# First modulation in four column steps, ten units computed chunk by chunk, in a one-core fp32 decoder layer

## The chip, the core and the metric

The kernel runs on one core of a Trainium2 chip. The metric is the device time of the whole program in microseconds (us). PE is TensorE, ACT ScalarE, DVE VectorE, POOL GpSimd, SP the engine whose queue issues most transfers. A number such as L1267 is a line of the kernel.

## What is computed

One decoder layer, 256 tokens (`S`) of 1024 features (`D`), all float32. A modulation vector of 6 x 1024 numbers comes from `c`; its first third (shift and scale) acts on the normalised input of the mixer. The mixer projects that input by `w_in` (6216 columns) into queries, keys and values of three attention branches, an indexer and gates.

```python
c_act = jax.nn.silu(c)
mod = c_act @ w_ada[l] + b_ada[l]
sh1, sc1, g1, sh2, sc2, g2 = [m[:, None, :] for m in jnp.split(mod, 6, axis=-1)]
h = rms_norm(x, g_pre_mix[l]) * (1.0 + sc1) + sh1
y = hybrid_mixer(h, w_in[l], b_gate[l], w_proj_sb[l], w_proj_moba[l], w_proj_dsa[l], w_o[l], slopes)
x = x + g1 * rms_norm(y, g_post_mix[l])
h = rms_norm(x, g_pre_ffn[l]) * (1.0 + sc2) + sh2
y = swiglu(h, w_up[l], w_down[l])
x = x + g2 * rms_norm(y, g_post_ffn[l])
```

In the mixer: 5 heads of plain causal attention (`mb`), 6 of stick-breaking attention (`sb`), 5 that see only the 64 keys with the highest index score (`ds`); the scores come from 8 small index heads ("logits").

## The kernel before

**Precision.** Every weight and activation is cut into a high part (an ACT copy to fp32r) and a low part (a DVE subtraction), and a product is three matmuls: high x high, high x low, low x high (`three`, L1265 to L1269). So each weight block that arrives costs ACT and DVE one pass each (`cut_hi` L635, `cut_lo` L931) before PE can use it.

**Mixer units.** `w_in` is loaded in 17 column blocks (all 1024 rows each) through two buffers `raw[0]` and `raw[1]`; block b may be loaded when block b-2 has been cut. The 51 units of `UNITS` are the output tiles: unit 0 (block 0, index keys and weights), 1 to 4 (block 1, index queries), 5 and 6 (block 2, queries of mb), 7 to 9 (block 3, keys of mb and a last head), 10 and 11 (block 4, values), and so on to the 24 gate units 27 to 50. A unit of features takes 24 matmuls: 8 chunks of 128 input features, three matmuls each. Each engine runs through the units in program order, and tables by unit number place everything else between them: `LOGIT_PAIR_AT` (index logits), `ROUND_AT` (eight top-k rounds on DVE), `SCORES_AT`, `EXP_AT`, `SECOND_AT`, `OUTPUT_AT` (attention of one head every two units), `ADA_UNIT` (the other two thirds of the modulation: 16 parts of 1 MB, loaded by POOL and accumulated on DVE at L1001 to L1007), `PIECES_AT` (the cuts of block b+1 during the units of block b).

**Start.** The first third of the modulation needs 8 MB of `w_ada`: a quarter of its rows at a time goes to `raw[0]`, `raw[1]` and two `ada_end` buffers, all issued by SP ahead of `w_in`. PE multiplies it (L1274), DVE copies the row (L1013), PE turns it (L1307), DVE makes scale and shift columns, ACT and DVE apply them to the turned x (L734, L1038) and cut the result (L738, L1046), and unit 0 starts. All 2048 sums end with the last rows.

**Tail of the mixer.** Blocks 17 to 20 are the projection weights; SP may issue block 19 (L461, L466) only after the last cut of block 17, which stands at unit 50. Then POOL merges the branches (L604, L607), `w_o`, and the feed-forward loop.

## Time and profile before

| | |
|---|---|
| median of 3 runs | 475.29 us (472.71 to 476.57) |
| the profiled execution: its own time | 475.56 us |
| its span in the trace | 473.4 us |
| mean granted TensorE clock | 0.983 of full |

The profile shows one execution. Its span is 2.2 us shorter than its own time, by what lies ahead of and behind the traced work. Rows of the trace are in a section below; a start time in them is counted from the beginning of the span.

### The profile page before, as it was taken

How to read it: one execution, taken by the hardware profiler on the slowest of the kernel's cores; microseconds unless marked ns; L12 is line 12 of the kernel's file. 1: busy time of each engine (PE TensorE's matmuls, PEld its weight loads, DVE VectorE, ACT ScalarE, POOL GpSimd, SP SyncE). 2: the span in 40 equal slices, each digit the busy share in tenths (PEclk: the TensorE clock that was granted, in tenths of full speed). 3: DMA queues.
4: the chain of work that ended last, by engine and by line, in shares of the span. 5: the costliest groups of instructions: out<-in, count | busy, mean ns of one | idle time of the engine just before them, and what ended most of it. 6: DMA issues, size and time to landing. Idle time of an engine off the chain costs nothing.

```text
span 473.4 us, 7656 instructions
## 1 busy us (share of the span) xinstructions
PE 442.6 (93%) x2927; PEld 390.4 (82%) x2927; DVE 315.3 (67%) x542; ACT 237.4 (50%) x417; POOL 55.0 (12%) x84
## 2 busy tenths in 40 slices
PE   0959999999999999999988999999999999999994
PEld 0629999999889999998886899888888888888883
DVE  3047579768399959673799447785855675585545
ACT  6046555546576655567465237554444253444232
POOL 2001001200023140000399100000000000000000
PEclk9969999999999999999999999999999999999998
DMA  8996898596856675752677900998475556620002
GB/s 296 426 367 212 271 312 298 180 316 226 325 182 206 238 267 206 251 162 76 198 267 280 369 17 2 329 362 271 133 237 177 190 164 200 237 94 1 1 0 89
DMA packets 56817, 99.85 MB, mean 211 GB/s; under 512 B 5212, under 2 KB 41684, under 8 KB 53716
## 3 DMA queue, kind: packets, MB, share of 16 engines
q1 hardware_dynamic: 54132, 81.62, 50.3%
q0 software_dynamic: 2656, 17.84, 10.7%
q8 instruction: 19, 0.31, 0.3%
q14 instruction: 10, 0.08, 0.0%
HBM read 98.39 MB, written 1.06 MB: 210 GB/s over the span
## 4 chain that ended last, share of the span: by engine, by line
PE 81%; DMA 5%; POOL 4%; DVE 3%; ACT 2%; SPq 2%; issue 1%; DVEq 0%; POOLq 0%; PEldq 0%; ACTq 0%
PE psum L1267 16%; PE psum L1567 16%; PE psum L1268 15%; PE psum L1269 15%; PE psum L1568 8%; DMA ada_end<-in_w_ada_dram 4%; PE psum L1531 3%; DVE wlo L931 1%; POOL xn L607 1%; POOL bufp L604 1%; PE psum L1418 1%; POOL hcut L598 1%; PE psum L1357 1%; PE psum L1355 1%; PE psum L1389 1%
## 5 line engine op out<-in xcount | busy, mean ns | idle before, releaser
L1567 PE MATMUL psum<-hcut,whi 128*128 128x512 f32 x320 | 111.9, 395 | 0.0
L1267 PE MATMUL psum<-hcut,whi 128*128 128x256 f32 (+1 forms) x360 | 106.0, 294 | 3.5 <-DVE hcut L1046 2.7
L1268 PE MATMUL psum<-hcut,whi 128*128 128x256 f32 (+1 forms) x360 | 102.4, 284 | 0.0
L1269 PE MATMUL psum<-hcut,wlo 128*128 128x256 f32 (+1 forms) x360 | 102.3, 284 | 0.0
L931 DVE TENSOR_TENSOR wlo<-raw,whi 128x1024 fp32r<-128x1024 f32 (+4 forms) x84 | 78.0, 957 | 24.6 <-ACT whi L635 24.3
L1568 PE MATMUL psum<-hcut,wlo 128*128 128x256 f32 x320 | 88.9, 278 | 0.0
L635 ACT ACTIVATE whi<-raw 128x1024 fp32r<-128x1024 f32 (+4 forms) x84 | 66.3, 821 | 22.7 <-DMA raw<-in_w_in_dram 16.5
L1267 PEld LDWEIGHTS psum<-hcut,whi 128*128 128x128 f32 (+1 forms) x360 | 68.9, 191 | 8.6 <-issue 3.2
L1567 PEld LDWEIGHTS psum<-hcut,whi 128*128 128x128 f32 x320 | 60.0, 188 | 14.1
L1268 PEld LDWEIGHTS psum<-hcut,whi 128*128 128x128 f32 (+1 forms) x360 | 69.0, 192 | 0.0
L1269 PEld LDWEIGHTS psum<-hcut,wlo 128*128 128x128 f32 (+1 forms) x360 | 68.9, 191 | 0.0
L1568 PEld LDWEIGHTS psum<-hcut,wlo 128*128 128x128 f32 x320 | 60.1, 188 | 0.4
L1196 DVE TENSOR_TENSOR dlo<-draw,dhi 128x2048 fp32r<-128x2048 f32 x11 | 25.1, 2291 | 44.0 <-ACT dhi L840 44.0
L1191 DVE TENSOR_TENSOR wlo<-raw,whi 128x1024 fp32r<-128x1024 f32 x40 | 47.1, 1220 | 4.5 <-ACT whi L833 4.5
L833 ACT ACTIVATE whi<-raw 128x1024 fp32r<-128x1024 f32 x40 | 39.8, 1046 | 3.1 <-DMA raw<-in_w_up_dram 3.1
L1007 DVE SCALAR_TENSOR_TENSOR acc<-xn,csil,acc 128x2048 f32<-128x2048 f32 x14 | 32.9, 2350 | 7.0 <-DMA xn<-in_w_ada_dram 6.9
L840 ACT ACTIVATE dhi<-draw 128x2048 fp32r<-128x2048 f32 x11 | 20.9, 1912 | 31.1 <-PE psum L1269 31.1
L878 ACT ACTIVATE fsil<-fsil 128x256 f32<-128x256 f32 x20 | 8.4, 418 | 52.8 <-DVE fsil L1208 52.8
L1268 PE MATMUL psum<-dlo,fhi 128*128 128x512 f32 x88 | 34.3, 390 | 0.0
L1267 PE MATMUL psum<-dhi,fhi 128*128 128x512 f32 x88 | 34.3, 390 | 0.0
L1269 PE MATMUL psum<-dhi,flo 128*128 128x512 f32 x88 | 34.3, 390 | 0.0
L1268 PE MATMUL psum<-wlo,hcut 128*128 128x320 f32 (+2 forms) x80 | 28.2, 353 | 0.0
(180 smaller groups left out, 697.8 us busy)
## 6 DMA issues: line engine op xcount, KB each, us to landing
raw<-in_w_up_dram SPq DMA_DIRECT2D x22, 1024.0 KB, 7.5
xn<-in_w_ada_dram POOLq DMA_DIRECT2D x16, 1024.0 KB, 5.2
raw<-in_w_in_dram SPq DMA_DIRECT2D x7, 2048.0 KB, 9.1
draw<-in_w_down_dram SPq DMA_DIRECT2D x11, 1024.0 KB, 5.1
raw<-in_w_in_dram SPq DMA_DIRECT2D x4, 1280.0 KB, 7.1
raw<-in_w_in_dram SPq DMA_DIRECT2D x3, 1536.0 KB, 7.0
raw<-in_w_ada_dram SPq DMA_DIRECT2D x2, 2048.0 KB, 9.8
ada_end<-in_w_ada_dram SPq DMA_DIRECT2D x4, 1024.0 KB, 17.0
```

Source lines behind the costliest of these rows:

```text
L635: act.activation(block_view(whi[b % 2], b)[0:p, chunks, cols], block_view(raw[r % 2], b)[0:p, chunks, cols], ACT.Copy).then_inc(w_hi, 1)
L833: act.activation(block_view(whi[slot], B_FFN)[:, 2 * q:2 * q + 2, :], block_view(raw[slot], B_FFN)[:, 2 * q:2 * q + 2, :], ACT.Copy).then_ ...
L840: act.activation(dhi[slot][:, :, :], draw[slot][:, :, :], ACT.Copy).then_inc(d_hi, 1)
L931: dve.tensor_tensor(block_view(wlo[b % 2], b)[0:p, chunks, cols], block_view(raw[r % 2], b)[0:p, chunks, cols], block_view(whi[b % 2], b)[ ...
L1007: ins = dve.scalar_tensor_tensor(acc[:, :], ada_part, csil[:, k:k + 1], acc[:, :], ALU.mult, ALU.add)
L1191: dve.tensor_tensor(block_view(wlo[slot], B_FFN)[:, 2 * q:2 * q + 2, :], block_view(raw[slot], B_FFN)[:, 2 * q:2 * q + 2, :], block_view(w ...
L1196: dve.tensor_tensor(dlo[slot][:, :, :], draw[slot][:, :, :], dhi[slot][:, :, :].bitcast(F32), ALU.subtract).then_inc(d_lo, 1)
L1267: pe.matmul(dst, a[0], b[0], start=first, stop=False)
L1268: pe.matmul(dst, a[0], b[1], start=False, stop=False)
L1269: return pe.matmul(dst, a[1], b[0], start=False, stop=last)
L1567: pe.matmul(dst[:, :], wh, hcut[:, k, :, :].rearrange("p a s -> p (a s)"), start=k == 0, stop=False)
L1568: mm = pe.matmul(dst[:, S:2 * S], wl, hhi[:, k, :], start=False, stop=k == KC - 1)
```

## The change

The first third of the modulation is now made in four steps p of 256 features. The sum of a feature runs over all rows of `w_ada`, so a step loads all 1024 rows of 2 x 256 columns (`load_ada`, 2 MB in pieces of 1 KB). Between the steps SP loads, for each chunk k of 128 input features, the rows of blocks 0 to 3 that belong to it (`load_chunk`: 1224 columns, 627 KB in rows of 2336, 1024 and 256 bytes). PE computes units 0 to 9 side by side: for each chunk three matmuls for each of ten units, in halves of banks 0 to 4. x is now turned without its norm; 1/rms is applied as a row (`rootrow`) together with the scale. Small vectors are loaded from ACT's queue instead of SP's. The copies of units 0 to 9 out of the banks, and the four logit pairs, come after the last chunk; heads start one unit later, and the tables of sums and top-k rounds are new. A helper `warm_up` (transposes of a constant) is defined and not called.

```diff
+FIRST_BLOCK, FIRST_UNIT = 4, 10
+Q_COLS, CHUNK_COLS = W_IX + HD + H_IX, W_IX + HD + H_IX + 2 * W_MB
+CHUNK_BASE = [W_IX, 0, Q_COLS, Q_COLS + W_MB - HD]
...
-HEAD_START = 13
+HEAD_START = 14
...
-LOGITS_AT = {5 + h: h for h in range(H_IX)}
-LOGIT_PAIR_AT = {5 + 2 * j: j for j in range(H_IX // 2)}
+LOGIT_PAIR_AT = {FIRST_UNIT + j: j for j in range(H_IX // 2)}
 TOPK_ROUNDS = TOPK // 8
-ROUND_AT = {25 + r: r for r in range(TOPK_ROUNDS)}
+ROUND_AT = {u: r for r, u in enumerate([18, 19, 24, 28, 29, 30, 32, 34])}
...
-    for b in range(N_MIX):
+    for b in range(FIRST_BLOCK, N_MIX):
...
-ADA_UNIT = [2, 4, 6, 9, 12, 15, 18, 22, 25, 28, 31, 34, 37, 40, 43, 46]
+ADA_UNIT = [12, 14, 16, 19, 21, 23, 25, 27, 29, 31, 33, 35, 37, 41, 43, 45]
...
+        def first_place(u):
+
+            return bank[u // 2][:, S * (u % 2):S * (u % 2 + 1)]
+
+        def mod_columns(p):
+
+            return bank[6 + p % 2][:, 0:4]
...
+            def load_ada(p):
+
+                if p >= 2:
+                    sp.wait_ge(gemv, p - 1)
+                for a in range(2):
+                    sp.dma_start(ada[p % 2][:, :, a, :], ada_dram[:, :, D * a + 2 * P * p:D * a + 2 * P * (p + 1)]).then_inc(ada_in[p], 16)
+
+            def load_chunk(k):
+
+                if k >= 6:
+                    sp.wait_ge(w_hi, 2 * (k - 2))
+                    sp.wait_ge(w_lo, 2 * (k - 2))
+                view = chunk_view(raw, None, k)
+                sp.dma_start(view[:, 0:Q_COLS], in_dram[:, k, O_QIX:O_QIX + Q_COLS]).then_inc(chunk_in[k], 16)
+                heads = in_dram[:, k, O_QMB:O_QMB + 2 * W_MB].rearrange("p (a n) -> p a n", a=2)
+                pairs, last = view[:, Q_COLS:CHUNK_COLS - P], view[:, CHUNK_COLS - P:CHUNK_COLS]
+                sp.dma_start(pairs.rearrange("p (a n) -> p a n", a=2), heads[:, :, 0:W_MB - HD]).then_inc(chunk_in[k], 16)
+                sp.dma_start(last.rearrange("p (a n) -> p a n", a=2), heads[:, :, W_MB - HD:W_MB]).then_inc(chunk_in[k], 16)
+
...
+                if b < FIRST_BLOCK + 2:
+
+                    sp.wait_ge(w_hi, (6, 2 * KC)[b - FIRST_BLOCK])
+                    sp.wait_ge(w_lo, (6, 2 * KC)[b - FIRST_BLOCK])
+                else:
+                    sp.wait_ge(w_hi, 4 * (b - 1))
+                    sp.wait_ge(w_lo, 4 * (b - 1))
...
+            for k in range(KC):
+                if k % 2 == 0:
+                    load_ada(k // 2)
+                load_chunk(k)
+            for b in range(FIRST_BLOCK, B_FFN):
+                load(b)
...
-                    pool.wait_ge(h_lo, 4)
+                    pool.wait_ge(tmp_ready, KC)
...
+                    if b < FIRST_BLOCK + 2:
+                        act.wait_ge(chunk_done, 3 * (b - FIRST_BLOCK + 1))
...
+            for w, k0 in ((b_ada, VEC_ADA), (g_pre_mix, VEC_PRE_MIX), (b_gate, VEC_GATE),
+                          (g_post_mix, VEC_POST_MIX), (g_pre_ffn, VEC_PRE_FFN), (g_post_ffn, VEC_POST_FFN)):
+                n = w.shape[0] * w.shape[1] // P
+                act.dma_start(vec_rows[k0:k0 + n, :], w.rearrange("l (k p) -> (l k) p", p=P)).then_inc(vec_in, 16)
...
+            act.wait_ge(x_in[0], 16)
+            act.activation(squares0[0], xt[:, 0, :], ACT.Square, accum_out=ssq[:, 0, 0:1]).then_inc(ss_ready, 2)
+            for i in (0, 2):
+                act.wait_ge(x_raw_turned, i + 1)
+                act.activation(h32[:, 2 * i:2 * i + 2, :], turned_two(i), ACT.Copy).then_inc(x_kept_act, 1)
+            act.wait_ge(var_ready, 2)
+            act.activation(root_[:, 0:TT], var[:, 0:TT], ACT.Sqrt).then_inc(sqrt_ready, 2)
+            for k in range(KC):
+                act.wait_ge(chunk_in[k], 48)
+                act.activation(chunk_view(whi, end_hi, k), chunk_view(raw, None, k), ACT.Copy).then_inc(w_hi, 2)
+                if k % 2 == 0:
+                    act.wait_ge(gemv, k // 2 + 1)
+                    if k:
+                        act.wait_ge(mod_turned, k // 2)
+                    act.activation(mrow[:, :], bank[5][:, :], ACT.Copy).then_inc(row_kept, 1)
+                act.wait_ge(tmp_ready, k + 1)
+                act.activation(hhi[:, k, :], htmp[k % 2], ACT.Identity, bias=col[0][:, k:k + 1]).then_inc(chunk_hi, 1)
+                if k == 1:
+                    act.preload_act_table_set("natural_log_exp_and_others")
+                cut_hi(FIRST_BLOCK, q)
+            for u in range(FIRST_UNIT):
+                take_unit(u)
+            for u in range(FIRST_UNIT, N_UNITS):
...
+            def chunk_cut_lo(k):
+                dve.wait_ge(w_hi, 2 * (k + 1))
+                dve.tensor_tensor(chunk_view(wlo, end_lo, k), chunk_view(raw, None, k),
+                                  chunk_view(whi, end_hi, k).bitcast(F32), ALU.subtract).then_inc(w_lo, 2)
+            def pair_columns(p):
+                dve.wait_ge(mod_turned, p + 1)
+                cols = slice(2 * p, 2 * p + 2)
+                scale, base = col[0][:, KC:2 * KC][:, cols], VEC_ADA + KC + 2 * p
+                then(dve.tensor_tensor(scale, mod_columns(p)[:, 2:4], vecs[:, base:base + 2], ALU.add))
+                then(dve.tensor_tensor(scale, scale, vecs[:, VEC_PRE_MIX + 2 * p:VEC_PRE_MIX + 2 * p + 2], ALU.mult))
+                then(dve.tensor_tensor(col[0][:, cols], mod_columns(p)[:, 0:2], vecs[:, VEC_ADA + 2 * p:VEC_ADA + 2 * p + 2], ALU.add))
+                dve.sem_inc(mod_ready, 1)
+            def chunk_scaled(k):
...
+                if k >= 2:
+                    dve.wait_ge(chunk_hi, k - 1)
+                dve.scalar_tensor_tensor(htmp[k % 2], h32[:, k, :], col[0][:, KC + k:KC + k + 1], rootrow,
+                                         ALU.mult, ALU.mult).then_inc(tmp_ready, 1)
+            def chunk_rest(k):
+                dve.wait_ge(chunk_hi, k + 1)
+                dve.scalar_tensor_tensor(hlo[:, k, :], htmp[k % 2], col[0][:, k:k + 1], hhi[:, k, :].bitcast(F32),
+                                         ALU.add, ALU.subtract).then_inc(chunk_lo, 1)
+            for k in range(KC):
+                chunk_cut_lo(k)
+                if k % 2 == 0:
+                    pair_columns(k // 2)
+                chunk_scaled(k)
+                chunk_rest(k)
+            dve.sem_inc(col_ready, 1)
+                cut_lo(FIRST_BLOCK, q)
...
-            def first_products():
-                for k in range(KC):
...
-                    mm = product(k, buf[:, ADA_COLS * (k % 2):ADA_COLS * (k % 2 + 1)])
...
+            def row_products(p):
+                pe.wait_ge(ada_in[p], 32)
+                if p == 0:
+                    pe.wait_ge(c_ready, 2)
+                else:
+                    pe.wait_ge(row_kept, p)
+                w = ada[p % 2]
+                for half in range(2):
+                    for j in range(4):
+                        mm = pe.matmul(bank[5][32 * j:32 * j + 32, :], crep[:, 4 * half + j, :],
+                                       w[:, 4 * half + j, :, :].rearrange("p a n -> p (a n)"),
+                                       start=half == 0, stop=half == 1, tile_position=(0, 32 * j))
+                mm.then_inc(gemv, 1)
+            def turn_row(p):
+                pe.wait_ge(row_kept, p + 1)
+                if p == 0:
+                    pe.wait_ge(pick_ready, 1)
+                    pe.wait_ge(x_kept_act, 1)
+                if p < 2:
+                    pe.wait_ge(x_kept_dve, 1)
+                else:
+                    pe.wait_ge(mod_ready, p - 1)
+                for n in range(4):
+                    mm = pe.matmul(mod_columns(p)[:, n:n + 1], mrow[:, P * n:P * (n + 1)], pick[:, :], start=True, stop=True)
+                mm.then_inc(mod_turned, 1)
...
+            def first_unit(u, k):
+                b, what, c0, n, dest = UNITS[u]
+                base = CHUNK_COLS - P if what == "last head" else CHUNK_BASE[b] + c0
+                wh, wl = [chunk_view(x, ends, k)[:, base:base + n] for x, ends in ((whi, end_hi), (wlo, end_lo))]
+                dst = first_place(u)[0:n, :]
+                pe.matmul(dst, wh, hhi[:, k, :], start=k == 0 and u in (1, 2, 4, 6, 8), stop=False, skip_group_check=True)
+                pe.matmul(dst, wh, hlo[:, k, :], start=False, stop=False, skip_group_check=True)
+                return pe.matmul(dst, wl, hhi[:, k, :], start=False, stop=k == KC - 1, skip_group_check=True)
...
+                if u < FIRST_UNIT + 2:
+                    pe.wait_ge(unit_read, 2 * (u - FIRST_UNIT + 1))
...
+            for i in range(4):
+                turn_raw_x(i)
+            pe.transpose(bank[4][:, 0:VEC_END], vec_rows[:, :], ident[0:VEC_END, 0:VEC_END]).then_inc(vec_turned, 1)
+            row_products(0)
+            pe.wait_ge(root_ready, 1)
+                mm = pe.transpose(bank[3][:, S + P * t:S + P * (t + 1)], rinv[:, t:t + 1].to_broadcast([P, P]), ident[:, :])
+            mm.then_inc(root_turned, 1)
+            turn_row(0)
+            for k in range(KC):
+                pe.wait_ge(w_hi, 2 * (k + 1))
+                pe.wait_ge(w_lo, 2 * (k + 1))
+                pe.wait_ge(chunk_hi, k + 1)
+                pe.wait_ge(chunk_lo, k + 1)
+                for n in range(FIRST_UNIT):
+                    u = n ^ 1 if k == 0 and n < 2 else n
...
+                    mm = first_unit(u, k)
+                    if k == KC - 1:
+                        mm.then_inc(units, 1)
+                    elif n == FIRST_UNIT - 1:
+                        mm.then_inc(chunk_done, 1)
+                    if n == 1 and k % 2 and k < KC - 1:
+                        turn_row(k // 2 + 1)
+                if k % 2 == 0 and k < KC - 2:
+                    row_products(k // 2 + 1)
...
+                        pe.wait_ge(unit_read, 8)
+                    if j == 1:
+                        pe.wait_ge(unit_read, 10)
```

What the order of instructions shows. On PE, from the last turned tile to the first unit, before (xn and ident hold the diagonal and identity, raw and ada_end the modulation weights, crep silu(c), mrow the summed row, hcut the cut input, whi and wlo the weight parts):

```order
L1324 MATMUL psum<-xn,xt 128x128 x16
L1274 MATMUL psum<-raw,crep 32x512 x16
L1274 MATMUL psum<-ada_end,crep 32x512 x16
L1307 MATMUL psum<-ident,mrow 128x128 x4
L1267 MATMUL psum<-hcut,whi 72x256
L1268 MATMUL psum<-hcut,whi 72x256
L1269 MATMUL psum<-hcut,wlo 72x256
```

And in the changed kernel on PE, from the last unit of chunk 0 to the third unit of chunk 1:

```order
L1401 MATMUL psum<-hcut,whi 128x256
L1402 MATMUL psum<-hcut,whi 128x256
L1403 MATMUL psum<-hcut,wlo 128x256
L1362 MATMUL psum<-ada,crep 32x512 x8
L1401 MATMUL psum<-hcut,whi 72x256
L1402 MATMUL psum<-hcut,whi 72x256
L1403 MATMUL psum<-hcut,wlo 72x256
L1401 MATMUL psum<-hcut,whi 128x256
L1402 MATMUL psum<-hcut,whi 128x256
L1403 MATMUL psum<-hcut,wlo 128x256
L1378 MATMUL psum<-pick,mrow 128x1 x4
```

The 32 products that stood in one piece ahead of all units are four groups of 8; the next step's group follows an even chunk, and its turn (L1378) stands behind two units of the odd chunk, so that eight units remain behind it.

On ACT, chunks 1 and 2 of the changed kernel (before, the ten copies of units stood among the cuts and no unit waited for them in one piece):

```order
L768 ACTIVATE whi<-raw 128x1224
L775 ACTIVATE hcut<-bufp,col 128x256
L777 ACT_TABLE_LOAD
L768 ACTIVATE whi<-raw 128x1224
L773 ACTIVATE mrow<-psum 128x512
L775 ACTIVATE hcut<-bufp,col 128x256
```

The copy of the row (L773) stands behind the cut of the chunk (L768), which waits for that chunk's arrival.

On SP, the first step and its two chunks in the changed kernel, up to the next step:

```order
L467 DMA ada<-in_w_ada_dram 128x8x256 x2
L475 DMA raw<-in_w_in_dram 128x584
L478 DMA raw<-in_w_in_dram 128x2x256
L479 DMA raw<-in_w_in_dram 128x2x64
L475 DMA raw<-in_w_in_dram 128x584
L478 DMA raw<-in_w_in_dram 128x2x256
L479 DMA raw<-in_w_in_dram 128x2x64
L467 DMA ada<-in_w_ada_dram 128x8x256 x2
```

Before, six whole transfers of `w_ada` stood here, and `w_in` behind all of them.

## Rows read from the trace of the kernel before

**Rows 1.** The page: busy time, slices of PE, chain by engine.

```profile
PE 442.6 (93%) x2927; PEld 390.4 (82%) x2927; DVE 315.3 (67%) x542; ACT 237.4 (50%) x417; POOL 55.0 (12%) x84
...
PE   0959999999999999999988999999999999999994
...
PE 81%; DMA 5%; POOL 4%; DVE 3%; ACT 2%; SPq 2%; issue 1%; DVEq 0%; POOLq 0%; PEldq 0%; ACTq 0%
```

**Rows 2.** Timeline of PE, 0 to 75 us: start, time, engine, line, tiles.

```profile
11.66 6.16 PE L1324 MATMUL psum<-xn,xt 128*128 128x128 f32 x32 [4.09 <-DVE xn L957]
17.75 3.64 PE L1274 MATMUL psum<-raw,crep 128*32 128x512 f32 x32
...
27.01 1.93 PE L1274 MATMUL psum<-ada_end,crep 128*32 128x512 f32 x8 [1.52 <-DMA ada_end<-in_w_ada_dram]
29.85 1.11 PE L1307 MATMUL psum<-ident,mrow 128*128 128x128 f32 x4 [0.91 <-DVE mrow L1013]
33.66 0.46 PE L1267 MATMUL psum<-hcut,whi 128*72 128x256 f32 x1 [2.70 <-DVE hcut L1046]
...
68.08 0.41 PE L1267 MATMUL psum<-whi,hcut 128*128 128x320 f32 x1
```

**Rows 3.** The chain that ended last, pieces of 0 to 54 and 214 to 262 us.

```profile
1.27 0.42 SPq L432
...
6.94 20.03 DMA ada_end<-in_w_ada_dram
...
53.52 0.42 PE psum L1355 x4
53.94 0.43 PE psum L1357 x4
...
220.01 1.59 ACT qk L803
221.59 0.53 ACT whi L635
...
223.53 0.37 SPq L461
```

**Rows 4.** Stretches: start:end, length, busy (x instructions) by engine, PEclk, DMA share, GB/s.

```profile
8.00:26.00 18.00, 12.52 (x88) 7.58 (x88) 2.58 (x13) 2.26 (x6) 0.00 (x0) 1.00 1.01 423
26.80:33.60 6.80, 3.05 (x12) 0.91 (x12) 3.67 (x11) 2.93 (x8) 0.00 (x0) 0.50 1.07 368
33.66:37.05 3.39, 3.38 (x16) 3.39 (x17) 2.79 (x5) 3.33 (x7) 0.00 (x0) 0.50 0.64 206
34.00:35.00 1.00, 1.00 (x7) 1.00 (x6) 1.00 (x2) 0.97 (x3) 0.00 (x0) 0.50 1.10 353
37.05:68.08 31.03, 30.73 (x253) 28.85 (x251) 22.15 (x28) 17.27 (x33) 2.28 (x4) 1.00 0.83 276
46.00:48.00 2.00, 2.00 (x19) 2.00 (x18) 0.23 (x2) 0.20 (x1) 0.00 (x0) 1.00 1.24 343
60.00:80.00 20.00, 20.00 (x157) 18.54 (x156) 16.30 (x23) 10.96 (x22) 1.05 (x2) 1.00 0.86 287
140.00:160.00 20.00, 20.00 (x159) 18.44 (x158) 19.65 (x44) 12.28 (x22) 5.32 (x15) 1.00 0.73 252
```

**Rows 5.** Who waited for whom, PE alone, 68 to 220 us.

```profile
PE psum L1267 <- DVE wlo L931: 0.5, 1, 0.5
```

**Rows 6.** Timeline of ACT, 0 to 75 us.

```profile
32.70 0.55 ACT L734 ACTIVATE xn<-psum,col 128x256 f32<-128x256 f32 x1
...
36.05 3.89 ACT L635 ACTIVATE whi<-raw 128x1024 fp32r<-128x1024 f32 x4
```

**Rows 7.** Timeline of DVE, 0 to 75 us.

```profile
29.10 0.69 DVE L1013 COPY mrow<-psum 128x512 f32<-128x512 f32 x1 [17.12 <-PEq L1290]
...
31.21 0.17 DVE L987 SCALAR_TENSOR_TENSOR col<-col,vecs 128x8 f32<-128x8 f32 x1
...
37.12 5.23 DVE L931 TENSOR_TENSOR wlo<-raw,whi 128x1024 fp32r<-128x1024 f32 x5 [0.26 <-ACT whi L635]
...
53.11 2.35 DVE L1007 SCALAR_TENSOR_TENSOR acc<-xn,csil,acc 128x2048 f32<-128x2048 f32 x1 [3.69 <-DMA xn<-in_w_ada_dram]
```

More of the change, by code:

```diff
@@ L1032, in _ @@
[L1032 to L1047 removed]
+            dve.wait_ge(ident_ready, 1)
```

327 lines of the change are left out of this document (143 added, 184 removed).

## The prediction, made before the changed kernel ran

> **What bounds the kernel now.** I read the page first. PE is busy for 442.6 of 473.4 us, its slices show 9 everywhere but at the start, around 220 to 260 us and at the end, and 81% of the chain that ended last is PE [rows 1]. So time can only be won where PE waits. I then read PE's timeline of the start, to see what stands ahead of the first unit: PE turns x, multiplies the first modulation as its parts arrive, and begins unit 0 at 33.66; the first block that the change leaves alone (unit 10) begins at 68.08 [rows 2]. The chain says why: a transfer of `w_ada` issued at 6.94 lands 20.03 later, at 26.97 [rows 3], and behind it come the last products, the copy of the row, its turn and the columns, 6.7 us to the first unit [rows 2]. The stretches show the queue full meanwhile (8 to 26 us: DMA share 1.01, 423 GB/s) and TensorE's granted clock: 0.50, its 1.2 GHz level, from 26.8 until 37.05, after thin work on PE (3.05 us busy of 6.8) and until unit 0 had kept it busy for 3.39 us; from then on 1.00, 2.4 GHz [rows 4]. Last I asked who PE waits for from 68 to 220 us: 0.5 us in all [rows 5]. What reaches unit 10 earlier therefore arrives earlier at 220 us too, unless something else becomes late.
>
> **What the change does to the start: transfers.** The same 8.39 MB of `w_ada` and 5.01 MB of `w_in` must arrive before unit 9 can end, but products and units now run beside the transfers. The price of the pieces changes. `w_ada` came in rows of 8 KB at 423 GB/s; pieces of 1 KB moved at 353 (34 to 35 us, block 2), and a mixture with pieces of 256 bytes at 343 (46 to 48 us) [rows 4]. I take 353 for the steps and 343 for the chunks: 2.10 MB / 353 = 5.9 us a step, 0.627 MB / 343 = 1.8 us a chunk, 4 x 5.9 + 8 x 1.8 = 38.4 us. SP issues x at 1.27 [rows 3]; x (1.05 MB) is through at about 5, and I add 1 us from last byte to landing. Arrivals: step 0 at 11.9, chunks 0 and 1 at 13.8 and 15.6, step 1 at 21.5, chunk 2 at 23.4, step 2 at 31.1, chunk 4 at 33.0, step 3 at 40.8, chunk 6 at 42.6, chunk 7 at 44.4. The waits of SP (`gemv`, cuts of chunks 3 and 4) are met before the queue runs dry, and the small vectors are on ACT's queue. The slow bound is 287 GB/s, the mean of 60 to 80 us with DMA share 0.86 [rows 4]: 46.7 us instead of 38.4.
>
> **The first chunk.** Behind chunk 0 at 13.8 stand the cut of 1224 columns (ACT, 4 cuts of 1024 took 3.89: 1.2 us [rows 6]), the copy of the row (DVE took 0.69 [rows 7]; ACT the same, I take 0.7), four turns of one column (no such row; four transposes at the low clock took 1.11 [rows 2]; bounds 0.4 and 1.1, I take 0.8), three small columns on DVE (0.17 and a semaphore each [rows 7]: 0.7), then scaled, high, low part (three of about 0.5, as L734's 0.55 [rows 6]) and handovers of 0.2: PE starts chunk 0 at about 19.
>
> **PE from there.** 240 matmuls. At the low clock 16 took 3.39 us, 0.21 each, at the high one about 0.12 (1.00 shows 253 records in 31.03 us, which hold three logit pairs too) [rows 4]: 28.8 us, and 1.5 more for a first 3.4 us at 1.2 GHz, since PE has idled before chunk 0. Three of the four product groups now stand in this stretch: 32 records took 3.64 [rows 2], so 16 take 1.8, together 5.5. Three turns at 0.7: 2.1. Sum 37.9: PE ends unit 9 at 19 + 37.9 = 56.9. Whether PE waits in between: the turn of step 1 needs chunk 2 (23.4), its cut, the products (26.1) and the copy (26.8), and PE reaches it at 26.8; the 24 matmuls behind it (2.9 us) cover columns, scale, cut and rest (2.3). For step 2 the same reckoning gives row and PE both at 36.6, for step 3 46.3 and 46.3. Transfers and PE are in balance, so each microsecond by which transfers are later costs most of a microsecond. In one chunk ACT works 1.2 + 0.5 + 0.35 = 2.1 us and DVE 1.4 (five cuts took 5.23 [rows 7]) + 1.0 + 0.35 = 2.8, against PE's 4.7: hidden; if the low parts of a chunk were late, PE would stand for the difference.
>
> **Behind the last chunk.** Block 4 comes after chunk 7 (1.31 MB, 3.8 us: 48.2) and is cut by 56; unit 10 waits for two copies only, the others (about 5 us of ACT) are done at 60.5, before the second logit pair asks for all ten at 65. Block 5 is issued when chunk 7 is cut (51.5), shares the queue with the first 1 MB part and is there by 60; its last low cut ends near 66.7, unit 12 asks for it about then. Unit 10 starts at 57.0. But three logit pairs, 0.42 + 0.43 each [rows 3], that stood ahead of 68.08, and the turn of the index weights (0.25), now stand behind: 2.8 us. Compared like with like the start wins 68.1 - 57.0 - 2.8 = 8.3 us.
>
> **What moves into the middle.** Four parts of the modulation (2.35 each on DVE [rows 7], the first less) and five logit sums leave the first ten units and are added to units 10 to 45: some 12 us of DVE work. Before, DVE had 16.3 of 20 us in 60 to 80 and 19.65 of 20 in 140 to 160, and there too PE did not idle [rows 4]. Over 36 units of some 3.7 us (133 us) that is 9 points more of DVE's time in the mean, and more ahead of unit 28, where three of the eight top-k rounds now stand as well; in return 140 to 160 us gets lighter. A part of 1 MB has 7.4 us for its load now. I charge 0.5 us; the bound above is the work that finds no room, 5 us.
>
> **The tail.** Heads are a unit later, so the last output stands at unit 49. On ACT its copy (0.4 and a wait of 0.8) comes between unit 49's copy and the sigmoid batch (1.59), and behind that is the cut (0.53) that lets SP issue block 19 at 223.53 [rows 3]. That is 1.2 later after unit 49, but PE comes to unit 49 0.8 earlier: +0.4.
>
> **Sum.** 473.4 - 8.3 + 0.5 + 0.4 = 466.0 of span, plus the 2.2 around it 468.2; the profiled execution is 0.3 above the median of the runs shown, so I say **468.0**, 1.5% less.
>
> **A rule against it.** The trace shows the low clock after thin work on PE [rows 4]. The Trainium skill, page "TensorE: Matmul & The Clock Gate", section "HAM oscillation — how this bites in real kernels", says that a matmul kernel which waits for a transfer behind each group of matmuls starts every group at the low clock again. By the row, the clock is low once, for 3.4 us; by the rule, each chunk pays, which is the first rival's result.
>
> **Rivals.** (1) *The clock stays low, slower.* Nothing keeps PE busy before chunk 0 and while rows are awaited. If all 240 matmuls and the groups ran at 1.2 GHz: 240 x 0.09 = 21.6 less the 1.5 counted, and 3 x 2 us of products (8 records took 1.93 at the low clock [rows 2]), +26: 494. It decides from three chunks at the low clock on (2.7 each: 476). For it: low clock after 3.05 of 6.8 us busy. Against: at 1.2 GHz a chunk takes 6.4 us, longer than its share of transfers (4.8), so PE would be busy all the time, and the row shows the rise after 3.4 such us. 0.10, with all other ways to be slower 0.12. (2) *Transfers bind.* At 287 GB/s everything is 8.3 us later and the start wins about 1: 475; at 320 GB/s 4 us are lost: 471.5. For it: many pieces of 1 KB and 256 bytes with the short rows of `w_in`; against: 353 and 343 were measured with such pieces. 0.15. (3) *Given back.* DVE finds no room in units 16 to 34, or the tail eats more: 470.5 to 474. For it: 19.65 of 20; against: 0.5 us of waits. 0.13. (4) The forecast and what lies near or below it (clock high at once, turns for 0.4: 464): 0.60.
>
> **How the numbers follow.** The forecast's own range is 464 to 471. Up to 475.5 come the transfers' and the middle's cases; below 463.5 I leave 0.06, above 475.5 0.13. About 1% (4.8 us) is what a measurement of this kernel can tell. Faster than 470.5: most of the forecast's cases, some of (3) and (2): 0.68. Slower than 480: 0.10. The rest, 0.22, within.
>
> **What would show it.** Right: the first L1401 near 19 us, unit 10 near 57, GB/s of 340 to 360 from 5 to 44, PEclk 0.5 for one stretch of some 3.4 us at chunk 0, block 19 issued near 216, the low cut with waits under 1 us on PE. Wrong: the first chunk behind 21; landings of steps more than 7 us apart beyond their two chunks; PEclk 0.5 in several chunks; PE waiting for `wlo` between 90 and 150 us, or the gap from unit 50 to the projections grown by more than 1 us.

## The result, and the profile after

The changed kernel takes 486.14 us (median of four runs, 483.34 to 488.63) against 475.93 us for the kernel before on the same chip: the ratio is 1.021, with a 95% interval of 1.012 to 1.031. It is slower by about 10 us where I had forecast 468.0. A second set of four runs of it gave 484.38 us and 1.021 (1.015 to 1.026). The profiled execution is the slowest of the first four (488.63 us), so the stretches below add up to somewhat more than the medians differ by.

The page of the changed kernel answers to [rows 1]: busy time, the slices of TensorE and of its granted clock, then the chain that ended last by engine.

```profile
PE 452.0 (93%) x2941; PEld 395.8 (81%) x2941; DVE 321.5 (66%) x550; ACT 237.8 (49%) x408; POOL 56.2 (12%) x84
...
PE   3699999999799997999979899989999999999994
...
PEclk9689999999979999999979999999999999999998
...
PE 58%; DMA 18%; DVE 13%; issue 4%; POOL 3%; ACT 3%; SPq 2%; DVEq 0%; ACTq 0%; POOLq 0%
```

The start fills its slices sooner (3, 6, 9 where there was 0, 9, 5), but the chain has changed character. 81% of it was PE; now it is 58% PE, 18% transfers and 13% DVE. There are also new 7s, where PE stands, in slices that were all 8s and 9s.

To see where the 13.5 us of span (486.9 against 473.4) arise, take three milestones: ACT's copies of units 14 and 50, and PE's first matmul by `w_up`, the up matrix of the feed-forward loop. Each fence holds rows of the timelines of ACT and PE, the first for the kernel before.

```profile
86.12 0.38 ACT L698 ACTIVATE qk<-psum 128x256 f32<-128x256 f32 x1 [2.81 <-PE psum L1269]
...
222.84 0.47 ACT L707 ACTIVATE qk<-psum,vecs 128x256 f32<-128x256 f32 x1 [0.73 <-PE psum L1269]
...
278.40 1.83 PE L1531 MATMUL psum<-xn,raw 128*128 128x128 f32 x15
```

The same three in the changed kernel:

```profile
81.48 0.39 ACT L734 ACTIVATE qk<-psum 128x256 f32<-128x256 f32 x1 [1.47 <-PE psum L1350]
...
229.35 0.47 ACT L744 ACTIVATE qk<-psum,vecs 128x256 f32<-128x256 f32 x1 [0.57 <-PE psum L1350]
...
288.05 2.17 PE L1664 MATMUL psum<-xn,raw 128*128 128x128 f32 x18
```

At unit 14 the changed kernel is 4.6 us ahead, at unit 50 it is 6.5 us behind, at the next milestone 9.7 behind and at the end 13.5. So the start did win; the units between lost 11.1 us; 3.1 us went between unit 50 and the up matrix, and 3.8 behind it.

One of these microseconds is no gain. Heads start one unit later now, so the scores of the first head stand ahead of unit 14 in the kernel before and behind it in the changed one. At unit 15 both have done them, and the lead is 3.6 us. These are the two copies of unit 15, first before, then changed.

```profile
89.00 0.38 ACT L698 ACTIVATE qk<-psum 128x256 f32<-128x256 f32 x1 [0.16 <-PE psum L1269]
```

```profile
85.41 0.38 ACT L734 ACTIVATE qk<-psum 128x256 f32<-128x256 f32 x1 [2.07 <-PE psum L1350]
```

Like with like, then, the start won 3.6 us, less than half of the forecast 8.3, and the units up to 50 lost 10.1. In the second profile of the changed kernel (span 481.9) the same two numbers are 3.8 and 9.2.

Next, who waited. The rows are: engine, tile and line that waited, for whom, us in all, times, the longest. First PE from 68 to 220 us, which was 0.5 us in all before [rows 5]; then DVE from 60 to 262 us (before: 3.3 us in all, the longest 1.1).

```profile
PE psum L1348 <- DVE wlo L973: 5.9, 4, 3.0
PE psum L1506 <- DVE smax L1199: 0.8, 1, 0.8
```

```profile
DVE acc L1046 <- DMA xn<-in_w_ada_dram: 15.1, 8, 4.5
```

DVE stands 15.1 us in `accumulate`, waiting for parts of the modulation; PE stands for the low cuts (`wlo`) that DVE makes in the same order of instructions. How one leads to the other is shown by the chain from 57 to 150 us: start, duration, what.

```profile
110.41 2.31 DVE acc L1046
112.71 0.28 issue
113.00 7.76 DMA xn<-in_w_ada_dram
120.78 2.36 DVE acc L1046
123.14 0.28 issue
123.43 6.29 DMA xn<-in_w_ada_dram
129.75 2.35 DVE acc L1046
132.10 1.15 DVE wlo L973
133.38 0.55 PE psum L1348
```

This is a closed loop. The parts have one buffer, so the next part is issued only when the last is accumulated: 2.35 us of DVE, 0.28 us to issue, and a load of 5.1 us at best, 6.29 and 7.76 here, where a weight block is on the queue too. One turn takes 7.75 us or more. The new table asks for a part every two units, mostly, and two units take 7.6 us in the mean of units 14 to 50 of the kernel before (7.1 to 7.8 for most gate units). At 133.38 PE has waited 2.96 us for the low cut behind the accumulation.

Stretches of the changed kernel follow (start:end, length, busy time and instructions of PE, PEld, DVE, ACT, POOL, then PEclk, DMA share, GB/s). They answer to [rows 4].

```profile
4.00:48.00 44.00, 35.42 (x245) 28.05 (x249) 20.20 (x43) 19.06 (x26) 0.00 (x0) 0.88 1.07 347
...
21.50:26.76 5.26, 5.26 (x24) 5.26 (x25) 2.31 (x3) 3.27 (x4) 0.00 (x0) 0.50 1.10 345
26.85:61.20 34.35, 34.35 (x289) 29.46 (x289) 18.63 (x31) 14.84 (x26) 0.69 (x1) 1.00 0.80 259
...
132.66:139.50 6.84, 6.12 (x21) 4.61 (x22) 4.21 (x6) 3.14 (x6) 0.28 (x1) 0.51 0.92 293
245.30:252.10 6.80, 6.06 (x28) 6.09 (x29) 3.45 (x8) 2.01 (x5) 4.97 (x5) 0.50 0.75 266
```

Two waits of PE, 2.96 us before 133.38 and 2.99 before 246.04, each go with 6.8 us at 1.2 GHz. The clock falls some 0.8 us before the wait ends, and for the 6.0 us of work behind it a matmul of 256 columns starts every 0.21 us instead of every 0.12.

Last, PE's timeline of the start, beside [rows 2].

```profile
13.37 3.48 PE L1362 MATMUL psum<-ada,crep 128*32 128x512 f32 x16 [3.46 <-DMA ada<-in_w_ada_dram]
...
17.57 1.05 PE L1378 MATMUL psum<-pick,mrow 128*128 128x1 f32 x8 [0.36 <-ACT mrow L773]
21.50 0.55 PE L1401 MATMUL psum<-hcut,whi 128*128 128x256 f32 x1 [2.88 <-DVE hcut L1117]
...
27.58 1.93 PE L1362 MATMUL psum<-ada,crep 128*32 128x512 f32 x16
...
61.22 0.31 PE L1348 MATMUL psum<-whi,hcut 128*128 128x320 f32 x1
```

Chunk 0 starts at 21.50 and unit 10 at 61.22; I had said 19 and 57. A first chunk behind 21, and PE waiting for `wlo` between 90 and 150 us, are two of the signs of being wrong that the prediction names.

### The profile page after: what moved, and what is told of

It is laid out like the page before. It is cut to its first block, busy times and chain, and to the rows that moved or that the text cites. A ratio compares the mean times of both kernels' runs of the same rounds, so it can differ in the third digit from the quotient of the medians.

```text
span 486.9 us, 7727 instructions
## 1 busy us (share of the span) xinstructions
PE 452.0 (93%) x2941; PEld 395.8 (81%) x2941; DVE 321.5 (66%) x550; ACT 237.8 (49%) x408; POOL 56.2 (12%) x84
## 4 chain that ended last, share of the span: by engine, by line
PE 58%; DMA 18%; DVE 13%; issue 4%; POOL 3%; ACT 3%; SPq 2%; DVEq 0%; ACTq 0%; POOLq 0%
PE psum L1700 14%; DMA xn<-in_w_ada_dram 9%; PE psum L1348 8%; PE psum L1350 8%; PE psum L1349 8%; PE psum L1701 7%; DMA raw<-in_w_in_dram 4%; DVE acc L1046 3%; PE psum L1664 3%; DVE wlo L973 3%; DMA ada<-in_w_ada_dram 2%; DMA raw<-in_w_up_dram 2%; PE psum L1362 2%; PE psum L1401 2%; PE psum L1402 1%
## 5 line engine op out<-in xcount | busy, mean ns | idle before, releaser
L1700 PE MATMUL psum<-hcut,whi 128*128 128x512 f32 x320 | 113.6, 399 | 1.7 <-DVE wlo L1272 1.7
L1701 PE MATMUL psum<-hcut,wlo 128*128 128x256 f32 x320 | 89.9, 281 | 0.0
L1348 PE MATMUL psum<-hcut,whi 128*128 128x256 f32 x280 | 82.9, 296 | 4.9 <-DVE wlo L973 4.9
L973 DVE TENSOR_TENSOR wlo<-raw,whi 128x768 fp32r<-128x768 f32 (+3 forms) x68 | 66.2, 1000 | 22.8 <-ACT whi L672 22.2
L1349 PE MATMUL psum<-hcut,whi 128*128 128x256 f32 x280 | 79.6, 284 | 0.0
L1350 PE MATMUL psum<-hcut,wlo 128*128 128x256 f32 x280 | 79.6, 284 | 0.0
L1700 PEld LDWEIGHTS psum<-hcut,whi 128*128 128x128 f32 x320 | 60.1, 188 | 17.0 <-issue 2.1
L672 ACT ACTIVATE whi<-raw 128x768 fp32r<-128x768 f32 (+3 forms) x68 | 55.7, 851 | 16.9 <-DMA raw<-in_w_in_dram 9.7
L1348 PEld LDWEIGHTS psum<-hcut,whi 128*128 128x128 f32 x280 | 54.0, 193 | 9.3 <-issue 5.9
L1701 PEld LDWEIGHTS psum<-hcut,wlo 128*128 128x128 f32 x320 | 60.4, 189 | 0.3
L1349 PEld LDWEIGHTS psum<-hcut,whi 128*128 128x128 f32 x280 | 54.1, 193 | 0.0
L1350 PEld LDWEIGHTS psum<-hcut,wlo 128*128 128x128 f32 x280 | 54.0, 193 | 0.0
L1046 DVE SCALAR_TENSOR_TENSOR acc<-xn,csil,acc 128x2048 f32<-128x2048 f32 x14 | 32.9, 2350 | 15.1 <-DMA xn<-in_w_ada_dram 15.1
## 6 DMA issues: line engine op xcount, KB each, us to landing
raw<-in_w_in_dram SPq DMA_DIRECT2D x6, 2048.0 KB, 10.1
```

The lines of the kernel that those rows point to most:

```text
L672: act.activation(block_view(whi[b % 2], b)[0:p, chunks, cols], block_view(raw[b % 2], b)[0:p, chunks, cols], ACT.Copy).then_inc(w_hi, 1)
L973: dve.tensor_tensor(block_view(wlo[b % 2], b)[0:p, chunks, cols], block_view(raw[b % 2], b)[0:p, chunks, cols], block_view(whi[b % 2], b)[ ...
L1046: ins = dve.scalar_tensor_tensor(acc[:, :], ada_part, csil[:, k:k + 1], acc[:, :], ALU.mult, ALU.add)
L1348: pe.matmul(dst, a[0], b[0], start=first, stop=False)
L1349: pe.matmul(dst, a[0], b[1], start=False, stop=False)
L1350: return pe.matmul(dst, a[1], b[0], start=False, stop=last)
```

## The experiments

All times are medians, ratios are to the kernel before on the same chip in the same sitting, with their 95% intervals. Four sittings: the first four kernels, the next four, the next four, the last three. The first kernel, the four combined ones, the shifted one and the last have ten executions each, the others four. Where two intervals overlap, a difference between these two kernels is suggested and not shown.

| kernel | us | ratio | interval |
|---|---|---|---|
| accumulations that do not wait | 478.25 | 1.009 | 1.006 to 1.011 |
| before, with the new table | 485.23 | 1.022 | 1.019 to 1.025 |
| wide table | 481.11 | 1.015 | 1.010 to 1.021 |
| parts in halves | 482.59 | 1.017 | 1.013 to 1.022 |
| old addresses | 483.95 | 1.022 | 1.017 to 1.027 |
| first part later | 483.79 | 1.021 | 1.018 to 1.024 |
| no wait, no accumulation | 475.59 | 1.004 | 0.999 to 1.009 |
| warm-up | 482.77 | 1.017 | 1.014 to 1.021 |
| combined | 474.55 | 1.001 | 0.999 to 1.004 |
| combined, parts whole | 476.43 | 1.004 | 1.001 to 1.006 |
| the changed kernel again | 484.38 | 1.021 | 1.015 to 1.026 |
| before, addresses shifted | 476.68 | 1.004 | 1.002 to 1.006 |
| combined, no accumulation | 471.73 | 0.995 | 0.992 to 0.997 |
| combined, old top-k table | 477.19 | 1.004 | 1.001 to 1.008 |
| before, halves and warm-up | 473.78 | 1.000 | 0.997 to 1.003 |

**Is it the wait for parts?** The first kernel takes the wait away and leaves every load where it is.

```diff
-                dve.wait_ge(part_in, 16 * (n + 1))
+                if n == 2 * KC - 1:
+                    dve.wait_ge(part_in, 16 * 2 * KC)
-                    ... acc[:, :], ada_part, ...
+                    ... acc[:, :], stale, ...        (stale is xt; in load_part POOL waits for the part before)
```

> The changed kernel, but the sixteen accumulations read another buffer and do not wait for their part; every part is still loaded, at the same point and into the same buffer (the sums of the second and third modulation are left out of the result). Theory 'part loop': the wait of VectorE for parts (15.1 us) and TensorE's waits behind it (8.9 us on the low cuts, two spells of 6.8 us at the low clock) go; the span falls by 8 to 12 us, to 475 to 478 us, and the milestones of units 23 to 50 return to those of before or earlier. Rival 'clock and start': the loss has other causes and this kernel stays within 3 us of the changed one (484 to 487).

It took 478.25 us: the wait costs 1.2% or some 6 us, and what was left of PE's waits from 60 to 262 us in it is this.

```profile
PE psum L1351 <- DVE wlo L975: 3.5, 3, 2.2
PE psum L1351 <- POOL hcut L637: 2.4, 3, 1.0
```

The time fell as the theory of the loop says, but by less than the 8 to 12 us expected, and to just above the expected range: the kernel without any wait for parts is still slower than before. (Its own POOL waits of 17.3 us for parts, which the edit added, may cost it a little.)

**Does the table alone do it?** The second kernel is the kernel before with the new table, and with the one line that must follow it, the unit after which POOL stores a gain (both as in the changed kernel).

```diff
-ADA_UNIT = [2, 4, 6, 9, 12, 15, 18, 22, 25, 28, 31, 34, 37, 40, 43, 46]
+ADA_UNIT = [12, 14, 16, 19, 21, 23, 25, 27, 29, 31, 33, 35, 37, 41, 43, 45]
...
-                if u == ADA_UNIT[KC] + 3:
+                if u == max(GAIN_AT) + 1:
                     store_gain(1)
```

> The kernel before with one edit: the units after which parts are accumulated are those of the changed kernel (12, 14, 16, 19, ... 45 in place of 2, 4, 6, 9, ... 46). Theory 'part loop': two units (7.1 to 7.5 us) are less than accumulate, issue and load (2.35 + 0.28 + 5.1 us or more), so this table alone slows the kernel before by 5 to 12 us. Rival 'the table is harmless, the loss comes of the start as a whole': within 2 us of before.

It is 2.2% slower than before, as much as the whole change. In it PE waits 6.5 us for low cuts between 60 and 262 us, and DVE 13.4 us for parts. The new start is not needed for the loss; the table is enough. Its 2.2% hold the wait and the crowding of DVE's work together, since it moves four accumulations from the first ten units to later ones; later kernels without the wait, or without the accumulations, ask for each alone.

**Can the loop be given room?** Two ways: more units between parts, or a shorter loop.

```diff
-ADA_UNIT = [12, 14, 16, 19, 21, 23, 25, 27, 29, 31, 33, 35, 37, 41, 43, 45]
+ADA_UNIT = [10, 12, 15, 17, 20, 22, 25, 27, 29, 32, 34, 37, 39, 42, 44, 46]
```

> The changed kernel with the sixteen accumulations spread over units 10 to 46, two or three units apart in turn (8.9 us on average in place of 7.4). Theory 'part loop': most of the 15.1 us of VectorE's waits and of TensorE's 8.9 us go; 474 to 478 us. If a two-unit distance now and then is already too much, 479 to 482. Rival: no change (485 to 487).

```diff
+                for i in range(2):
+                    if n and i:
+                        pool.wait_ge(acc_done, 2 * n)
+                    c0 = ADA_COLS * (1 + n // KC) + HALF * i
+                    pool.dma_start(ada_part[:, HALF * i:HALF * (i + 1)], ada_dram[:, n % KC, c0:c0 + HALF]).then_inc(part_in[i], 16)
...
+                    dve.wait_ge(part_in[i], 16 * (n + 1))
+                    ... accumulates columns HALF * i to HALF * (i + 1)
```

> The changed kernel with every part loaded and accumulated in two halves of 4 KB a partition: the first half is loaded again while the second is accumulated, so that the loop accumulate, issue, load is shorter (an estimate of 1.2 + 0.3 + 3.5 to 4.5 us for each half, in place of 7.75) at the same table of units. Theory 'part loop': 475 to 480 us. Rival 'the load is late because of the queue's and the memory's traffic, not because of its one buffer': 484 to 487.

Each gained less than I expected, some 2 to 3 us by the ratios, with intervals that overlap that of the changed kernel: 481.11, in the upper of the two ranges I had given, and 482.59, above its range of 475 to 480. In the wide table every second distance is still two units, and DVE waits 11.3 us for parts; with halves it waits 6.0 us, but the low cuts still come late (PE 4.4 us). Both point the same way as the first two runs, though neither gain is clear of noise by itself, and neither is the whole cure.

**Where is the rest?** Four single suspicions. The addresses first: the one new small buffer, `pick`, moves all later buffers by 32 bytes a partition.

```diff
-        pick = sb("pick", [P, 1])
         ...
         ssum = sb("ssum", [P, 2, TT], scope=mix)
+        pick = sb("pick", [P, 1], scope=mix)
```

> The changed kernel with the one new small buffer (pick, 32 bytes a partition) moved behind the others, so that the later buffers lie at the addresses they had before; no instruction changes otherwise. In the changed kernel each of the eight middle steps of the up and down matrices takes 16.79 us against 16.57 before, with the same instructions, and with the old program text and the new table it takes 16.57. Theory 'addresses': the steps return to 16.57 and the kernel gains 1.8 to 2.3 us, to 483 to 485. Rival 'place of the instructions in the program, or something else': the steps stay at 16.79, time 485 to 487.

```diff
                     pool.wait_ge(tmp_ready, KC)
+                    pool.wait_ge(raw_in[(FIRST_BLOCK + 1) % 2], RAW_ARRIVED[FIRST_BLOCK + 1])
```

> The changed kernel with the first part's load held back until the second weight block (block 5) has landed, so that the two do not share the queues. The block then lands 3 to 4 us earlier than at 66.35 and VectorE's idle 6.75 us before its cuts shrink. Theory 'part loop is what binds from unit 12 on': VectorE is free again before unit 12 either way, and the time stays within 1.5 us of the changed kernel. Rival 'the late block starts the delay': 3 to 4 us faster.

The third is the kernel without wait, with `accumulate` reduced to its semaphore for all parts but the first.

> As the kernel that accumulates from another buffer without waiting (478.25), but with fifteen of the sixteen accumulations left out (15 times 2.35 us = 35 us of VectorE; all parts are still loaded; the sums of the second and third modulation are wrong by that). It asks where the rest of the start's gain goes: that kernel was 5.8 us ahead of before at unit 12 and 2.0 behind it at the end. Theory 'VectorE's work itself is crowded, since three accumulations and three logit pairs moved from before unit 10 to behind it': TensorE's waits for low cuts (3.5 us) go too, and the time is 472 to 475. Rival: these waits come of the block loads or of the top-k steps, and it stays at 477 to 479.

```diff
             turn_row(0)
+            warm_up(12)
             for k in range(KC):
```

> The changed kernel with twelve transposes of the identity on TensorE in its idle stretch before chunk 0 (18.6 to 21.5 us), into a bank that chunk 0 starts afresh. The granted clock is at its lower level (1.2 GHz) from 13.2 to 16.6 and from 20.0 to 26.85 us. Theory 'clock': the low stretch behind 21.5 shortens or goes; chunk 0's 30 matmuls run at the upper level, unit 10 starts 2 to 3 us earlier than at 61.3; but since the later part loop binds, the end gains 1 us or less (484.5 to 486.5). Rival: the low stretch stays as long and nothing moves.

Addresses: the steps of the feed-forward loop did return to 16.57 us each. The median, 483.95, lies in the expected range, but so does that of the kernel beside it with the new addresses (483.79), and the ratio did not fall (1.022). An interval of 1.017 to 1.027 cannot show 0.4%, so the price was open until a later run. First part later: block 5 is cut from 64.3 instead of 66.35 us and DVE's idle stretch shrinks from 6.75 to 3.82 us, but the time stays (ratio 1.021); the delay does not start there. No accumulation: 475.59, just above the expected 472 to 475 and a further 0.4% below the first kernel, with intervals that overlap; suggestive, and taken up again below. Warm-up: PE's timeline shows what it does.

```profile
19.07 1.51 PE L1384 MATMUL psum<-ident 128*128 128x128 f32 x12
22.16 0.36 PE L1401 MATMUL psum<-hcut,whi 128*128 128x256 f32 x1 [1.59 <-DVE hcut L1117]
22.36 0.28 PE L1402 MATMUL psum<-hcut,whi 128*128 128x256 f32 x1
```

Chunk 0's matmuls take 0.28 us from the first, 0.12 apart, where they took 0.41, 0.21 apart. Chunk 0 started 0.7 us later in that execution and its product group still came at 25.89 instead of 27.58. The time is 482.77, 0.4% less than the changed kernel and more than I expected. But the intervals overlap, so it is not shown that the gain reached the end.

**Together, and the other way round.** The combined kernel has the wide table, the halves, the warm-up and the old addresses. Beside it ran the same with whole parts, the changed kernel again, and the kernel before with 32 bytes put in.

> The changed kernel with four edits together: parts in two halves, accumulations spread over units 10 to 46, the small new buffer behind the others (buffers at their old addresses), and twelve transposes of the identity before chunk 0. Measured one by one against before, in ratio: the changed kernel 1.021, wide table 1.015, halves 1.017, warm 1.017, and the address edit restores 16.57 us per middle step (about 2 us). If the effects add up as far as the waits allow: part waits gone (6 us), warm 1.7 us, addresses 2 us, so 474 to 476, ratio 0.999 to 1.004. Theory 'the crowded VectorE is what is left': not clearly faster than before, since about 3 us of accumulation work moved behind unit 10 remain. Rival: once nothing waits for parts the start's 6 us show and it is 470 or less.

> As the previous kernel but each part loaded whole, as in the changed kernel. Theory 'part loop': one part still needs 7.75 us or more, so with a distance of 7.4 us at every second part it waits some 10 us on VectorE in all and is 1.5 to 3 us slower than with halves. Rival 'the waits fall into VectorE's slack once the table is wide': within 1 us of it.

> The changed kernel once more (one comment differs), on the same chip as the kernels beside it, as their yardstick: 484 to 487, ratio 1.019 to 1.026.

```diff
+        spare = sb("spare", [P, 1])
         crep = sb("crep", [P, KC, 32])
```

> The kernel before with one unused small buffer (32 bytes a partition) in the place where the changed kernel has its new one, and nothing else. Theory 'addresses': the middle steps of the up and down matrices take 16.79 in place of 16.57 us and the time rises by 1.8 to 2.3 us (ratio 1.004 to 1.005). Rival 'the addresses matter only together with the changed program': no difference (within 0.5 us).

The combined kernel takes 474.55 us and is level with before (0.999 to 1.004); with whole parts it is 0.3% slower than that, by intervals that overlap (0.999 to 1.004 and 1.001 to 1.006). So the ten microseconds of the loss go with four small edits, and the chunk-by-chunk start stays in place. DVE's wait for parts in the combined kernel is down to this:

```profile
DVE acc L1052 <- DMA xn<-in_w_ada_dram: 3.5, 5, 1.5
```

The shifted kernel settles the addresses: 32 unused bytes cost 0.4% (1.002 to 1.006), some 1.8 us. These are the groups of the longest matmuls from 325 to 455 us (line, engine, tiles, shapes, count, busy time, mean ns), first the kernel before, then the same with the 32 bytes, then the changed kernel.

```profile
L1567 PE MATMUL psum<-hcut,whi 128*128 128x512 f32 x253 | 88.1, 393 | 0.0
L1568 PE MATMUL psum<-hcut,wlo 128*128 128x256 f32 x253 | 70.1, 277 | 0.0
```

```profile
L1568 PE MATMUL psum<-hcut,whi 128*128 128x512 f32 x250 | 88.6, 398 | 0.0
L1569 PE MATMUL psum<-hcut,wlo 128*128 128x256 f32 x250 | 70.2, 281 | 0.0
```

```profile
L1700 PE MATMUL psum<-hcut,whi 128*128 128x512 f32 x253 | 89.6, 398 | 0.0
L1701 PE MATMUL psum<-hcut,wlo 128*128 128x256 f32 x254 | 71.3, 281 | 0.0
```

The instructions are the same and each is recorded 4 or 5 ns longer. From the first to the last start of a step's 64 up matmuls it is 10.98 us before and 11.17 with the 32 bytes, which makes most of a step's 16.79 us for 16.57.

**What still holds the combined kernel back.** In its profile it is 6.5 us ahead of before at unit 15 and 1.7 at unit 50, and its median is level with before. Three more runs asked why.

> The combined kernel (wide table, halves, warm-up, old addresses; ratio 1.001 to before) with fifteen of its sixteen accumulations left out, their waits for parts kept (the sums of the second and third modulation are wrong by that): about 33 us less work on VectorE. Theory 'VectorE's own work is crowded behind unit 10': TensorE's waits for low cuts (3.4 us) and for the wo low halves go and the start's gain shows at the end: 470 to 472.5, ratio 0.991 to 0.996. Rival 'the rest is lost to the order of heads and top-k or in the tail': 474 or more.

```diff
-ROUND_AT = {u: r for r, u in enumerate([18, 19, 24, 28, 29, 30, 32, 34])}
+ROUND_AT = {25 + r: r for r in range(TOPK_ROUNDS)}
```

> The combined kernel with the eight top-k rounds at the units where they stood before (25 to 32 in a row, in place of 18, 19, 24, 28, 29, 30, 32, 34). Theory 'VectorE is crowded between units 12 and 24': the wait of 2.2 us for a low cut at 129.6 us goes, 1 to 2 us faster (ratio 0.997 to 0.999). Rival 'the spread of the rounds is needed': the stretch of rounds in a row delays cuts and heads, and the time stays or rises by 1 to 3 us.

```diff
             turn_rows(0)
+            for _ in range(12):
+                pe.transpose(bank[1][:, 0:P], ident[:, :], ident[:, :])
             for u in range(N_UNITS):
```

> The kernel before with two edits that the runs point to: parts in two halves, and twelve transposes of the identity in TensorE's idle stretch ahead of unit 0 (where the granted clock is low from 26.8 to 37.05 us and 16 matmuls take 0.41 in place of 0.28 us). Theory 'clock': unit 0 starts at the upper level and the kernel gains 1.5 to 2 us, with up to 1 us more from VectorE's shorter waits for parts (6.9 us before unit 10 and 3.3 behind): 471.5 to 473, ratio 0.993 to 0.997. Rival: TensorE would have waited for VectorE's cuts in the first units anyway and nothing is gained (ratio 0.999 to 1.001).

Without its accumulations the combined kernel takes 471.73 us, 0.5% less than before, and 0.6% less than with them: the work itself costs 3 us. The two intervals (0.992 to 0.997 and 0.999 to 1.004) are apart, though measured in two sittings. In its trace PE waits 0.2 us for low cuts between 60 and 262 us. With the old top-k table the kernel is at 1.004 (1.001 to 1.008), with 4.7 us of waits for low cuts against 3.4. My guess that the spread of the rounds crowds DVE asked for 0.997 to 0.999 and was wrong; that the spread helps is not shown, since the interval overlaps that of the combined kernel. The kernel before gains nothing from halves and warm-up (1.000): chunk 0's counterpart, unit 0, then starts at 32.66 with matmuls of 0.28 us, and ACT's copy of unit 0 comes 1 us earlier, but the end does not move by an amount that can be measured. No version beat the kernel before with all of its work in place.

## Why the prediction was wrong

**The middle is the step that failed.** It reads: "A part of 1 MB has 7.4 us for its load now. I charge 0.5 us; the bound above is the work that finds no room, 5 us." The load is only one of three links in a loop through one buffer. 2.35 us of accumulation, 0.28 of issue and 5.1 to 7.8 of load make 7.75 to 10.4 us, and two units give 7.6 in the mean: even the best turn of the loop has no room. All three durations could be had from the trace of before, in whose table all but the first two distances are three units or four. I had also asked the wrong question of DVE, how much of its time is busy. It takes its instructions in order, so a wait for a part holds up the low cuts behind it even when DVE has time to spare. Between units 14 and 50 the profile has 11.1 us where I charged 0.5. Of it, 1.0 us is the first head's scores, which have only changed places. 6.7 us are PE's waits shown above. Some 2.5 to 3 us are the low clock behind 133.38, by an estimate from the rows: PE works for 6.0 us there, and at the upper level matmuls start 0.12 us apart instead of 0.21. That leaves less than 1 us in no wait that the trace names. The first experiment takes away the wait (6 us), and the last batch prices the work (3 us). So the theory "the work finds no room" was true too, and the smaller part.

**The start: right in kind, 3.6 us instead of 8.3.** The transfers were right: 347 GB/s from 4 to 48 us at a share of 1.07, as the prediction took 353 and 343, and PE waits for nothing from chunk 0 to unit 10. But step 0 landed at 13.3 (11.9 said), and the first product group took 3.48 us at the low clock, where I had let it run beside the cut for nothing: chunk 0 began at 21.5. From there to unit 10 PE took 39.7 us against 37.9. The terms were 1.93 us a group (1.8 said), 1.05 a turn (0.7 said; the trace records eight instructions for a turn), and a low clock for 5.3 us (3.4 said), which is 24 matmuls 0.09 us longer, 2.2 us.

**The clock at the chunks.** It was low once, as forecast, so rival (1) fell: 24 matmuls at 0.50, then 1.00 until 132 us. Later, PE's waits of 2.96 and 2.99 us go with 6.8 us at 0.50 each. That agrees with what the Trainium skill says, page "TensorE: Matmul & The Clock Gate", section "HAM oscillation — how this bites in real kernels": where matmuls come in groups and PE waits for a transfer between them, the next group starts slow. Here PE waits for a low cut, and it shows 70 us and more behind the chunks, where the prediction did not look for it.

**The tail: 0.4 said, 3.1 in the profiled execution, but not in general.** From unit 50's copy to the up matrix it took 58.7 us against 55.6. In the second profile of the changed kernel the same stretch took 55.5 (228.25 to 283.79). In the profiles of the other kernels it took 53.6 to 57.2 us. So the 2.99 us wait and the slow clock behind it belong to some executions; I do not count them as a cost of the change.

**The addresses were not in the prediction at all.** Of the 3.8 us lost behind the up matrix, 1.73 are one wait of PE for a low cut of the third up block, at 323.75, and most of the rest is the 0.22 us in each step. The diff showed a new buffer ahead of others; I had priced it at nothing without saying so. The wait at 323.75 stands in every trace of the new start but one (0.8 to 1.7 us; the kernel without wait and accumulation lacks it) and not in before's. Behind it is the load of that block: ACT can cut it 10.4 us after SP's issue (9.6 in the second profile), where before it was 8.3, and at 310 GB/s in between, not less than the 295 before. Why it lands later is open, and no run isolates it.

**The account.** From the ratios, taken at 474.4 us: waits for parts 5.9 us, accumulation work 2 to 3, addresses 1.8, low clock at the start 1.8. Together that is 11.5 to 12.5, against 12.4 between the changed kernel (1.021) and the combined one without accumulations (0.995). Each term is uncertain by 1 to 3 us and the last is not clear of noise, so that the sum fits is partly luck. The last kernel is 2.5 us ahead of before where 7.4 were forecast (8.3 less 0.5 and 0.4), and not even these 2.5 are the new start's alone: 1.8 may be the warm-up's, and fifteen accumulations that the kernel before does are left out. With all of its work in place, the new start shows no gain at the end. In the profile of that last kernel it is 4.8 us ahead at unit 50, 5.8 at the up matrix and 4.8 at the end, but that execution was the fastest of its ten.

**The chances.** I gave "given back" 0.13 and put it at 470.5 to 474, and all slower cases 0.12. Its mechanism, work that finds no room on DVE, was the smaller part of what came (3 us), and its size at most 6 us against 10.1, since its price was bounded by DVE's busy time and not by the loop. The wait of DVE for its parts stands in none of the rivals.

## What to carry to other kernels

When a change packs a repeated load into fewer places, add up the whole loop through its buffer (use, issue, load, at the transfer's loaded duration, not at its best) and compare it with the distance between two uses. Half a part at a time shortens the loop without a byte more of memory: it took DVE's waits for parts from 15.1 to 6.0 us, and the time by 2 us or so, not clear of noise. A second whole buffer was not tried. On an engine that takes instructions in order, the price of a late transfer is that of whatever stands behind the waiting instruction, and the busy share says nothing of it. And keep buffer addresses in mind when two versions are compared: a small new buffer in front of large ones moved this kernel by 0.4%.

## What was not expected of the hardware

A shift of 32 bytes a partition in the addresses of buffers that the matmuls themselves do not read (`hcut`, `whi` and `wlo` lie ahead of the new buffer and kept theirs) makes float32 matmuls of 512 and 256 columns 4 or 5 ns longer each, 16.79 us a step instead of 16.57. It comes with the shift in the kernel before and goes with it in the changed one. What moved are the buffers that DVE, ACT and the loads of `w_down` use at the same time, and the down matmuls' own operands. The Trainium skill, page "SBUF — State Buffer", section "SBUF: two separate sides", says that TensorE's port never waits for another engine. By that rule the accesses of the other engines, wherever they lie, should not lengthen these matmuls. The measurement shows that the step does depend on those addresses, and through which accesses stays open.

A granted clock of 1.00 near the start can mean that there is no record. In the kernel without wait and accumulation the view says 1.00 for the stretch of chunk 0, while its first 13 matmuls start 0.21 us apart, the spacing of the lower level. The trace of that run holds its first clock record at 25.4 us, which is where the spacing shortens to 0.12; ahead of it the view fills in 1.00. In the kernel before the first record stands at 16.6 us, so the 1.00 of its stretch from 8 to 26 us [rows 4] rests on a record only from there. For the start, the spacing of the matmuls is the better witness. These are that kernel's stretch (columns as above) and two rows of its timeline of PE:

```profile
21.50:26.76 5.26, 4.33 (x25) 4.36 (x26) 2.80 (x4) 3.26 (x5) 0.00 (x0) 1.00 1.10 346
```

```profile
22.99 0.41 PE L1401 MATMUL psum<-hcut,wlo 128*128 128x256 f32 x1
23.20 0.41 PE L1399 MATMUL psum<-hcut,whi 128*72 128x256 f32 x1
```
